# Attention of a decoder layer: transposing products two pair steps behind the scores, value products three

## What is computed

```python
s_c = einsum(q, k_cmp) * scale + bias_c;  p_c = softmax(where(ok_c, s_c, NEG));  o_c = p_c @ v_cmp
s_s = einsum(q, k_g)   * scale + bias_s;  p_s = softmax(...);                    o_s = p_s @ v_g
s_w = einsum(q, k_w)   * scale + w_bias;  p_w = softmax(...);                    o_w = p_w @ v_w
o_nsa = gi[..., 0:1] * o_c + gi[..., 1:2] * o_s + gi[..., 2:3] * o_w
# MLA heads, causal:
s = (einsum(qn, k_nope) + einsum(qr, k_rope)) * scale;  o_mla = softmax(where(kpos <= t, s, NEG)) @ v
```

## Time and profile before

| | |
|---|---|
| median of three runs | 1833.64 us |
| the profiled execution | 1826.97 us |
| its span | 1824.9 us |
| attend in that span | about 165 to 358 us |
| TensorE busy over the span | 93% |
| VectorE, ScalarE busy over the span | 74%, 35% |

### The profile page before, as it was taken

How to read it: one execution, slowest core, us unless ns; L and a number is a source line. 1 busy time by engine, 2 the same in 40 slices (tenths; PEclk the granted TensorE clock), 3 DMA queues, 4 the chain that set the end, 5 groups by cost and what they waited for, 6 DMA issues and landing times. The chain is left out here.

```text
span 1824.9 us, 26553 instructions
## 1 busy us (share of the span) xinstructions
PE 1694.7 (93%) x8905; PEld 1347.1 (74%) x8905; DVE 1345.1 (74%) x3357; ACT 629.9 (35%) x998; POOL 323.2 (18%) x305
## 2 busy tenths in 40 slices
PE   7999899896989999999875999999999998999997
PEld 6877566676865566665474999898788887888885
DVE  3455676545779799779389888587788887888887
ACT  3433454522210122222032444456333333333333
POOL 0100020201001134443011322000322222222220
PEclk9987999898999999999888999999999999999999
DMA  6520000032216689887944897443999999999995
GB/s 229 204 93 24 1 2 1 14 129 81 92 46 212 206 265 313 286 301 240 351 149 147 269 300 253 146 128 118 338 322 322 323 320 325 306 322 319 324 321 203
DMA packets 215116, 380.76 MB, mean 209 GB/s; under 512 B 16707, under 2 KB 148099, under 8 KB 214892
## 3 DMA queue, kind: packets, MB, share of 16 engines
q1 hardware_dynamic: 159840, 226.40, 37.8%
q0 software_dynamic: 37952, 143.18, 22.7%
q10 hardware_dynamic: 17228, 9.98, 1.8%
HBM read 340.66 MB, written 41.98 MB: 210 GB/s over the span
## 5 line engine op out<-in xcount | busy, mean ns | idle before, releaser
L1811 PE MATMUL psum<-v_hi,wa_hi 128*128 128x512 f32 x768 | 301.2, 392 | 12.7 <-DVE wa_lo L1762 12.7
L1811 PE MATMUL psum<-v_lo,wa_hi 128*128 128x512 f32 x768 | 300.3, 391 | 0.0
L1811 PE MATMUL psum<-v_hi,wa_lo 128*128 128x512 f32 x768 | 300.3, 391 | 0.0
L1725 ACT ACTIVATE v_hi<-v_raw 128x1024 fp32r<-128x1024 f32 x126 | 133.7, 1061 | 312.8 <-PE psum L1811 231.1
L1394 POOL DMA_INDIRECT u_rows<-u,eid x128 | 157.2, 1228 | 421.7 <-DVE sdot L1516 386.1
L1705 POOL DMA_INDIRECT v_rows<-v,eid x128 | 131.1, 1024 | 540.6 <-DVE x_back L1773 377.7
L103 PE MATMUL psum<-h_hi,u_hi 128*128 128x384 f32 x512 | 180.2, 352 | 35.8 <-DVE u_lo L1522 35.8
L1599 PE MATMUL psum<-h_raw,u_raw 128*128 128x384 f32 x512 | 175.4, 500 | 15.4 <-ACT act_out L1410 8.2
L1811 PEld LDWEIGHTS psum<-v_hi,wa_hi 128*128 128x128 f32 x768 | 145.1, 189 | 44.9 <-DVE wa_lo L1762 10.0
L103 PE MATMUL psum<-h_lo,u_hi 128*128 128x384 f32 x512 | 175.1, 342 | 0.0
L103 PE MATMUL psum<-h_hi,u_lo 128*128 128x384 f32 x512 | 175.0, 342 | 0.0
(11 more groups left out here) (286 smaller groups left out, 2868.4 us busy)
## 6 DMA issues: line engine op xcount, KB each, us to landing
v_raw<-v SPq DMA_DIRECT2D x126, 512.0 KB, 5.2
u_raw<-uT SPq DMA_DIRECT2D x66, 512.0 KB, 4.7
v_first<-uT SPq DMA_DIRECT2D x62, 512.0 KB, 5.9
acts<-act_out SPq DMA_DIRECT2D x128, 192.0 KB, 3.4
acts_in<-acts SPq DMA_DIRECT2D x128, 192.0 KB, 4.2
wq_raw<-wq SPq DMA_DIRECT2D x16, 512.0 KB, 3.5
gates<-dense ACTq DMA_DIRECT2D x2, 4096.0 KB, 29.2
gates_in<-gates SPq DMA_DIRECT2D x128, 64.0 KB, 4.9
```

Of the source, the lines that this page charges most:

```text
L1725: act.activation(hi[:, c, :], raw[:, c, :], ACT.Copy).then_inc(vhi_ok, 1)
L1811: mm = pe.matmul(psum[:, 2 * t + b, :], w[:, c, ts], v[:, c, bs], start=(first and n == 0), stop=(last and n == 2), skip_group_check=True)
```

## The change

TensorE's order in a pair step p becomes: scores of pair p, turns of pair p - 2, values of pair p - 3, with one more pair step at the end. The copies follow their turns in the slots of VectorE and ScalarE (`TURN` 4 for 2), and the finishing too (`DRAIN` 7 for 5). `FACTOR`, the rings, the banks, the number and the shapes of all instructions stay.

```diff
-        FACTOR, TURN, DRAIN = 1, 2, 5
+        FACTOR, TURN, DRAIN = 1, 4, 7
...
-            for p in range(n_units // 2 + 2):
+            for p in range(n_units // 2 + 3):
                 if p < n_units // 2:
                     scores(2 * p)
                     scores(2 * p + 1)
-                if 1 <= p <= n_units // 2:
-                    turn(2 * p - 2)
-                    turn(2 * p - 1)
-                if p >= 2:
-                    values(2 * p - 4)
+                if 2 <= p < n_units // 2 + 2:
+                    turn(2 * p - 4)
+                    turn(2 * p - 3)
+                if p >= 3:
+                    values(2 * p - 6)
```

## The result

The changed kernel takes 1810.02 us, the median of four runs (1806.85 to 1815.22), against 1833.41 us for the kernel before in its four: the ratio is 0.9882, with a 95% interval of 0.9848 to 0.9916. A second measurement gave 0.9889 (0.9871 to 0.9906). So the change saves about 20 us (17 to 24 by the second interval). The forecast was 17.5 us less, 1816.1 us.

The account below looks back on a forecast made before the run. No engine but TensorE was near full, and it waited inside a pair step for VectorE's `scale`. Terms -20.6 + 1.6 + 1.5 = -17.5 us took 1833.64 to 1816.1 us; range 1810 to 1826.

Parts of the forecast that it names:

- The main term: Attention block: TensorE's turn loads no longer stall for VectorE's `scale`, 17.8 us plus 2.8 us in MLA units, 20.6 us less.
- more than forecast: Whole kernel at 1807 to 1811 us if the clock holds at b = 0 and (1) costs nothing; chance 0.04.
- (1): Exponential waits for a turn of its own step, delaying the second narrow turn in tiles 0 and 3; 1.6 us more.
- the forecast's own part: Whole kernel at 1811 to 1821 us; chance 0.64.
- (2): Pipeline one pair step deeper: an extra step without scores at the end, 1.5 us more; nothing back at the start.
- (3): Stretch with b = 0, clock partly at 1.2 GHz: counted as 0, with 3 us either way.
- The reason given for the stall: VectorE's slots: the second narrow unit's factor comes behind the first wide unit's scores' step; 1.09 us in tiles 0 and 3.
- A: Waits return smaller at the copies, 0.2 us for a bank or copy in each of 48 steps: 1824.1 us; chance 0.20.
- B: A buffer sets the period, so the stall only changes name and nothing is won: 1833.6 us; chance 0.07.
- C: Exponential's wait closes the ring of engines in every step, slower: 11.9 us more, 1845.5 us; chance 0.05.
- Period: Score-load starts should repeat every 5.9 us instead of 6.97 in tiles 0 and 3, and alike in tiles 1 and 2.
- Scores waiting for their banks: Sign that the prediction is wrong: score products in the block begin to wait for their banks; no size given.

Follow-up runs that it names:

- the experiments with the banks and the ring: Changed kernel with three PSUM banks for the turns, two for outputs: 1807.02 us; separately, changed kernel with a ring of 5 for `pr`: 1807.42 us.
- half of the change: Changed kernel with values two pair steps behind instead of three, turns still two: 1902.22 us, 1.0377 against the kernel before.
- both reliefs: Changed kernel with three PSUM banks for the turns (two for outputs) and a ring of 5 for `pr`: 1806.41 us, 0.9866 against the kernel before.
- each half of this change: Against the kernel before: only the turns moved, to two pair steps behind, 1902.22 us; only the values moved, to three, 1861.11 us.

## Why the prediction was right, and where it wasn't

**The place and the size of the gain.** The main term was 20.6 us of stalls for `scale`, read from the gaps between the two turns of a pair. By stretches, tiles 1 and 2 gave 9.24 for 9.0 and their MLA units 0.79 for 0.6; in the first half 10.74 for 9.3. The block as a whole gave 18.8 for 17.5, and the timed runs 19.3 to 23.4. The first median, 1810.02 us, lies at the very edge of the range (1810 to 1826), in the part that the prediction called more than forecast and gave 0.04; its reason for that part, a clock that holds and a term (1) of nothing, is not what happened. The second median, 1812.16 us, lies in the forecast's own part.

Two readings were off and partly cancel. The stall of the MLA units of tiles 0 and 3 was taken as 0.54 us a period from one period; the other three have 0.30, as this row of the kernel before:

```profile
247.57 0.30 PEld L764 LDWEIGHTS psum<-scale,pr 128*128 128x128 f32 x2 [0.30 <-DVE scale L886]
```

So that term was 0.7 us too large. And at the start of the block, where (2) expected nothing back, the way to the eighth pair's score loads became 5.0 us shorter (24.77 to 19.79), of which its two stalls of 1.09 explain 2.2; no experiment isolates the other 2.8. The same stretch of the second half, up to its seventh pair, gave 2.6 us (26.19 to 23.62) for the 2.3 of its two periods, so the 0 of (3) was good there.

**The nearer wait of the exponential (1).** The walk was good to 0.1 us: exponential 2.26 us after the start of the wide step, measured 2.32 (202.43 - 200.11); VectorE's wide copy from 3.53 to 4.22, measured 3.63 to 4.31, as these rows have it:

```profile
202.43 0.72 ACT L824 ACTIVATE pr<-sc,top 128x512 f32<-128x512 f32 x1 [2.40 <-PE psum L764]
...
203.74 0.68 DVE L721 COPY prT<-psum 128x512 f32<-128x512 f32 x1
```

The stall came in the kind of steps foreseen, six times instead of eight, with 0.38 us (0.29 with MLA) where the sum had 0.2: 2.0 us for 1.6. By the experiments with the banks and the ring the chain costs about 4 us in all; what it costs outside these six steps, mostly around b = 0 and partly by the clock there, the sum didn't have.

**The deeper pipeline (2).** 1.99 us for 1.5.

**The reason given for the stall.** Here the prediction said too much. It put the stall down to VectorE's order, the factor behind a score product that hasn't ended. The experiment with the factor ahead confirms this for the narrow turns, whose stall goes; but the wide turns then wait as long and the block grows by 7.3 us, because the exponential's time stands in VectorE's way instead. So the order only decides which turn waits; what has to be covered is the round trip of a pair through the engines, for which one pair step was too little. The forecast didn't hang on this, since the change lengthens the distance and doesn't touch the order.

**The rivals.** A (0.2 us in every one of 48 steps, 1824.1 us) didn't come: the wait is in 6 steps. B (a buffer sets the period) is refuted for the banks by the kernel before with a third one, 1.0004. A deeper ring of `pr` wasn't tried in the kernel before, but its exponentials wait for VectorE and not for a turn. The Trainium skill says in Perfetto Trace Analysis, Optimization Strategy, that consistent bubbles can mean too little SBUF or PSUM. That isn't so for the old bubble, by the 1.0004, and it is so for the new one: after the change the same edit to the banks took 4.5 us off the block. C (all engines in lockstep) didn't come with the full change, but it is what half of the change does: period 9.86 us, 1902 us.

**The signs named beforehand.** Loads waiting for scale: under 4 us asked, 3.8 found, in 4 places at the head and in the b = 0 stretch. Period: 5.9 asked, 6.05 found in tiles 0 and 3, 5.86 in tiles 1 and 2. Exponential released by the turn: found, 53.1 us. The b = 0 stretch didn't grow. Scores waiting for their banks, named as a sign of being wrong: once, 1.5 us at the start of the block (the last of the waits after the change), otherwise not beyond 0.3 us.

What stays open: what exactly the half clock in the stretches with b = 0 costs (it is 0.54 in 264 to 268 us of the changed kernel; with both reliefs, where it doesn't fall, the second half's stretch is 3.5 us shorter, but part of that is the shorter waits themselves), where the 2.8 us at the start come from, and why the rest of the program is several us longer in one execution than in another.

## What to carry to other kernels

When engines that work in order hand a tile round in a ring, look at the engine that ends the block. A gap that one and the same producer releases in every period, while no other engine is full, can ask for more distance between the steps. Another order is the rival to try: here VectorE's order only moved the gap (7.3 us worse), and TensorE's, with ready work put into the gap, won 10.7 of the 18.8 us. Move all stages behind the moved one by as much, or the ring can close inside a step: each half of this change alone cost 81 and 28.5 us of block. Then ask of each ring and bank whether its depth still exceeds the new distance; one slot more where it just doesn't was worth about 4 us here, and a third bank was worth nothing before the distance was there.

## What the hardware showed that I had not expected

A stall of TensorE can cost a second time, through the clock. With the granted clock at 1.00, sixteen loads of the wide turns took 1.86 us; in the two half changes some of the same groups took 3.36 and 3.43 us, at a granted clock of 0.50 (1.2 for 2.4 GHz). In the ten us before the fall TensorE's matmuls were never idle longer than 1.39 us in the first of them, and the next group ran at 1.00 again after waits of the same kind, so these traces don't tell which wait brings the clock down. The kernel before, whose weight loads were never idle longer than 1.02 us between 183 and 254 us, kept 1.00 through that stretch. I had priced the half changes too low (29 to 60 us for 100, 1832 to 1845 for 1861): the larger part is that the waits of a closed ring are longer than the gaps that I had added up, the smaller one the clock.
